# Output-gate projection of an mLSTM/S5 layer: plain float32 products replaced by three products of high and low parts

## The reference, cut to what matters

```python
xn = rmsnorm(h, norm1_g[l])
z = xn @ w_in[l]                       # 2048 x (4*1024 + 8 + 1024)
q, k, v, o, gates, u = jnp.split(z, [W, 2 * W, 3 * W, 4 * W, 4 * W + 2 * H], axis=-1)
qk = jax.nn.silu(causal_dwconv(jnp.concatenate([q, k], axis=-1), conv_qk_w[l]))
...
hm = mlstm_chunkwise(to_heads(q), to_heads(k), to_heads(v), li, lf)
hm = hm * lax.rsqrt(jnp.mean(hm * hm, axis=-1, keepdims=True) + RMS_EPS)
hm = hm.reshape(B, S, W) * mlstm_norm_g[l] * jax.nn.sigmoid(o)
ys = s5_groups(u, ...)
mix = jnp.concatenate([hm, ys], axis=-1) @ w_out[l]
```

## Time and profile before

| | us |
|---|---|
| median of 3 runs (lowest, highest) | 3444.53 (3444.41, 3446.69) |
| profiled execution, its own time | 3445.2 |
| its span | 3443.5 |
| busy: PE, DVE, ACT, POOL | 2603.8, 2528.7, 828.4, 1117.8 |

### The profile page before, as it was taken

How to read it: one execution, slowest core, us unless ns; L and a number is a source line. 1 busy time by engine, 2 the same in 40 slices (tenths; PEclk the granted TensorE clock), 3 DMA queues, 4 the chain that set the end, 5 groups by cost and what they waited for, 6 DMA issues and landing times. The chain is left out here.

```text
span 3443.5 us, 26884 instructions
## 1 busy us (share of the span) xinstructions
PE 2603.8 (76%) x10227; PEld 1778.2 (52%) x10227; DVE 2528.7 (73%) x2565; ACT 828.4 (24%) x794; POOL 1117.8 (32%) x654
## 2 busy tenths in 40 slices
PE   9999999625060600025558999999999999999999
PEld 4444674202020200012226888788788788888887
DVE  5997548889999999986676787679666544444565
ACT  2002231100000100000003333455433433333333
POOL 6550008786867687876660000000000000000000
PEclk9999999857575755557778999999999999999999
DMA  8885459999999999999997997454657555555775
GB/s 288 312 326 182 171 189 407 412 422 421 421 415 421 401 422 422 421 422 422 422 421 268 325 319 272 147 159 158 214 195 256 170 185 193 185 192 185 266 268 186
DMA packets 326003, 1023.36 MB, mean 297 GB/s; under 512 B 33784, under 2 KB 34312, under 8 KB 259212
## 3 DMA queue, kind: packets, MB, share of 16 engines
q1 hardware_dynamic: 251996, 484.97, 41.3%
q0 software_dynamic: 73904, 537.04, 37.6%
HBM read 1015.08 MB, written 6.86 MB: 297 GB/s over the span
## 5 line engine op out<-in xcount | busy, mean ns | idle before, releaser
L403 DVE TENSOR_TENSOR slab_low<-ring,slab_high 128x2048 fp32r<-128x2048 f32 x220 | 504.3, 2292 | 489.1 <-ACT slab_high L396 489.0
L396 ACT CAST slab_high<-ring 128x2048 fp32r<-128x2048 f32 x284 | 542.3, 1910 | 893.1 <-PE bank L382 722.8
L1996 POOL DMA_INDIRECT pool<-in_peer_u,pool x239 | 494.0, 2067 | 301.3 <-DVE pool L1722 202.0
L1772 DVE CUSTOM_DVE_ANT_0 pool<-pool,nat 128x2048 f32<-128x2048 f32 x235 | 535.0, 2291 | 42.9 <-DMA pool<-in_peer_u,pool 41.5
L380 PE MATMUL bank<-slab_high,left_high 128*128 128x512 f32 x1408 | 551.8, 392 | 11.7 <-DVE res L1810 6.3
L382 PE MATMUL bank<-slab_high,left_low 128*128 128x512 f32 x1408 | 549.6, 390 | 0.0
L381 PE MATMUL bank<-slab_low,left_high 128*128 128x512 f32 x1408 | 549.3, 390 | 0.0
L2507 PE MATMUL bank<-pool,causal 128*128 128x512 f32 x288 | 189.1, 818 | 424.3 <-ACT causal L2187 328.3
L1783 DVE SCALAR_TENSOR_TENSOR res<-pool,res 128x2048 f32<-128x2048 f32 x169 | 397.4, 2351 | 106.2 <-DMA pool<-in_peer_v,pool 92.7
L1996 POOL DMA_INDIRECT pool<-in_peer_v,pool x241 | 400.1, 1660 | 209.5 <-PE bank L2507 108.5
L2507 PEld LDWEIGHTS bank<-pool,causal 128*128 128x128 f32 x288 | 73.6, 266 | 538.2 <-issue 367.8
(11 more groups left out here) (628 smaller groups left out, 3341.0 us busy)
## 6 DMA issues: line engine op xcount, KB each, us to landing
ring<-in_w_in SPq DMA_DIRECT2D x141, 1024.0 KB, 5.2
ring<-in_w_ffn_in SPq DMA_DIRECT2D x88, 1024.0 KB, 5.0
ring<-in_w_ffn_out SPq DMA_DIRECT2D x44, 1024.0 KB, 5.1
nat<-in_w_ada SPq DMA_DIRECT2D x68, 512.0 KB, 5.6
ring<-in_w_out SPq DMA_DIRECT2D x32, 1024.0 KB, 5.1
left_scratch<-in_w_ada SPq DMA_DIRECT2D x60, 512.0 KB, 5.6
ring<-in_w_ada SPq DMA_DIRECT2D x23, 1024.0 KB, 5.5
ring<-in_peer_wq SPq DMA_DIRECT2D x10, 1024.0 KB, 5.1
```

Of the source, the lines that this page charges most:

```text
L396: nc.scalar.copy(high[:, n % PARTS], ring[:, g % SLOTS]).then_inc(high_done, 1)
L403: eng.tensor_tensor(dst, ring[:, g % SLOTS], high[:, n % PARTS].bitcast(F32), ALU.subtract)\
L1772: v.tensor_tensor_reduce(out=row, in0=row, in1=nat[:, t, :], scale=1.0, scalar=0.0, op0=ALU.mult, op1=ALU.add, accum_out=actv[:, t, m:m + ...
L1996: g.indirect_dma_start(dst, None, a[table][0], bass.IndirectOffsetOnAxis(idx[:, t, n:n + 1], 0))\
```

## The change

The eight slabs of the output gate are multiplied as three float32r products instead of plain float32.

- At the end of the first block ACT copies `raw_left` into a float32r array laid over `res` (two copies of 128 x 2048), and DVE subtracts it from `raw_left` in place (128 x 2048, 128 x 1024, 128 x 1024), each part once the last projection has read it. `left_high` so holds the low part of the left side.
- Each slab's high part is made in `slab_low` by a copy: slab 0 by ACT in the first block, slab 1 by POOL, slabs 2 to 7 by ACT, set between the other steps of its order.
- Each slab's low part is a subtraction on POOL, in place in the ring: slab 0 in the first block, the rest in the second.
- `res` is loaded again only when all eight slabs are used.

```diff
+        def o_high_part(eng, x):
+            g = O0 + x
+            eng.wait_ge(landed[slot_of(g)], reach[g])
+            if x >= PARTS:
+                eng.wait_ge(slabs_used, g - PARTS + 1)
+            if x == PARTS:
+                eng.wait_ge(low_done, x)
+            copy = nc.scalar.copy if eng is nc.scalar else nc.gpsimd.tensor_copy
+            copy(low[:, x % PARTS], slot(g)).then_inc(high_done, 1)
+
+        def o_low_part(x):
+            g = O0 + x
+            nc.gpsimd.wait_ge(high_done, x + 1)
+            nc.gpsimd.tensor_tensor(ring_low[:, slot_of(g)], slot(g), low[:, x % PARTS].bitcast(F32), ALU.subtract)\
+              .then_inc(low_done, 1)
...
 # first block, GpSimd, at its end
+                o_low_part(0)
 # first block, ScalarE, in front of taking the last projected block
+                            act.wait_ge(s_yp, SC)
+                            for ks in (slice(0, KD // 2), slice(KD // 2, KD)):
+                                nc.scalar.copy(o_left_high[:, ks, :], raw_left[:, ks, :]).then_inc(s_olh, 1)
+                            act.wait_ge(s_tab, SC)
+                            o_high_part(act, 0)
 # first block, VectorE, behind the scan
+                    for lo, hi in ((0, KD // 2), (KD // 2, KD - KS), (KD - KS, KD)):
+                        dve.wait_ge(s_olh, 1 if lo == 0 else 2)
+                        dve.wait_ge(slabs_used, place_of["in", (IN_BLOCKS - 3) * NB, hi // KS - 1] + 1)
+                        v.tensor_tensor(aTh[:, lo:hi, :], raw_left[:, lo:hi, :], o_left_high[:, lo:hi, :].bitcast(F32),
+                                        ALU.subtract)
 # second block, SyncE
-                stream_on(sp, O0, O0 + 4)
+                stream_on(sp, O0, len(front))
+                sp.wait_ge(slabs_used, len(front))
                 sp.dma_start(res, a["x"][0].rearrange("(t p) d -> p t d", p=P)).then_inc(s_x, 16)
-                stream_on(sp, O0 + 4, len(front))
                 sp.wait_ge(s_x, 16)
 # second block, GpSimd
+                o_high_part(g, 1)
+                o_low_part(1)
                 g.wait_ge(s_glub, 1)
                 g.wait_ge(s_cs, 1)
                 g.tensor_copy(condition, spread[:, :, 31]).then_inc(s_io, 1)
+                for x in range(PARTS, 8):
+                    o_low_part(x)
 # second block, ScalarE
                 for n in range(4, 8):
                     raw_copy(n)
-                for c in range(4):
+                o_high_part(act, 2)
+                for c in range(2):
+                    s5_sigmoid(c)
+                o_high_part(act, 3)
+                for c in range(2, 4):
                     s5_sigmoid(c)
...
+                o_high_part(act, 4)
                 for c in range(4, 6):
                     s5_sigmoid(c)
                 o_sigmoid(0)
+                o_high_part(act, 5)
                 for c in range(6, 8):
                     s5_sigmoid(c)
...
+                for x in range(6, 8):
+                    o_high_part(act, x)
                 act.wait_ge(s_m, mk["sq"])
 # second block, TensorE, o_slab(x)
-                    whole_slab(pe, O0 + x, [(ps[6 + t][:, :], t) for t in range(TT)], 4 * j, j == 0, j == 3)
+                    pe.wait_ge(low_done, x + 1)
+                    for k in range(KS):
+                        for t in range(TT):
+                            lh, ll = o_left(4 * j + k, t)
+                            hs, ls, into = low[:, x % PARTS, k, :], ring_low[:, slot_of(g), k, :], ps[6 + t][:, :]
+                            nc.tensor.matmul(into, lh, hs, start=j + k == 0, stop=False)
+                            nc.tensor.matmul(into, lh, ls, start=False, stop=False)
+                            last = nc.tensor.matmul(into, ll, hs, start=False, stop=(j, k) == (3, KS - 1))
+                    last.then_inc(slabs_used, 1)
```

More of the change, by code:

```diff
@@ L109, in build @@
         spare, _ = place_at("slab_low_scratch", PARTS * SLAB, F32, low_at)
-        res_, _ = place_at("res", TT * D)
+        res_, res_at = place_at("res", TT * D)
         aTh_, aT_at = place_at("left_high", KD * T, F32R)
@@ L216, in build @@
         place_of = {what: g for g, what in enumerate(front)}
+        O0 = place_of["in", (IN_BLOCKS - 2) * NB, 0]
         def front_slab(g, s):
@@ L278, in is_whole @@
             sec = max(i for i in range(len(SECTIONS)) if first_slab[i] <= g)
-            return sec in (FRONT, PEER_Q) or any(first_slab[i] <= g < first_slab[i] + WHOLE for i in (W_OUT, FFN_IN))
+            return g < O0 or sec == PEER_Q or any(first_slab[i] <= g < first_slab[i] + WHOLE for i in (W_OUT, FFN_IN))
         WHOLE = 2
@@ L288, in is_in_place @@
         def is_in_place(g):
-            return first_slab[GATES] <= g < first_slab[W_OUT2]
+            return first_slab[GATES] <= g < first_slab[W_OUT2] or O0 <= g < len(front)
         def split_index(g):
@@ L386, in left, with o_left @@
             return aTh[:, k, t * P:(t + 1) * P], aTl[:, k, t * P:(t + 1) * P]
+        o_left_high = view(place_at("o_left_high", KD * T, F32R, res_at)[0][:, :], [KD, T])
+        def o_left(k, t):
+            return o_left_high[:, k, t * P:(t + 1) * P], aTh[:, k, t * P:(t + 1) * P]
+        def o_high_part(eng, x):
[12 more added lines that the diff above has]
+              .then_inc(low_done, 1)
         def high_part(act, g, i=None):
@@ L597, in build @@
         U0 = place_of["in", C_U, 0]
+        s_olh = sem("o_left_high_copied")
         s_xp, s_rot, s_st, s_yp, s_yd = (sem("s5_inputs"), sem("s5_inputs_taken"), sem("s5_states"), sem("s5_outputs"),
@@ L600, in build @@
         s_proj, s_v5 = sem("qkv_taken"), sem("s5_vector_step")
-        O0 = place_of["in", (IN_BLOCKS - 2) * NB, 0]
         per_chunk = (O0 - S0) // SC
@@ L931, in s5 @@
                     for b in range(IN_BLOCKS - 2):
+                        if b == IN_BLOCKS - 3:
+                            act.wait_ge(s_yp, SC)
[3 more added lines that the diff above has]
+                            o_high_part(act, 0)
                         act.wait_ge(slabs_used, place_of["in", b * NB, 3] + 1)
```

## The result

The changed kernel takes 3457.99 us (median of 7 executions, 3456.17 to 3462.58) against 3444.41 of the kernel before on the same chip (7 executions, 3441.68 to 3446.69): a ratio of 1.0042, 95% interval 1.0033 to 1.0052. It is 13.6 us slower; 3457.4 was forecast. The profiled execution took 3457.99 with a span of 3456.3.

What follows compares the result with a forecast made beforehand. PE sets the pace, DVE close behind. Query-key products 15.1 us late less 4.3 returned (+10.8), restarts +1.5, first block +0.6: +12.9 on 3445.2 gives 3458.1, median 0.7 lower, 3457.4 us; 8-in-10 range 3442 to 3465.

Steps and rivals of the forecast that it cites:

- Rivals 1 and 2: 1: POOL doesn't hold DVE, 3436.2 us, chance 0.13; 2: two convolution low parts fall into DVE's waits or bank reads, 3448.2, 0.15.
- rival 3: Heavier: both restarts at the low clock, POOL's copy at 4.6 us, low parts at 5.5; about +20, 3465 us, chance 0.12.
- two restarts: PE resumes at the lower clock after waiting at `s5_glu(1)` and `s5_glu(6)`; +1.5 us together, range 0 to 3.7.
- Rival 4: PE waits for POOL's low parts themselves; no time beyond that of rival 3, chance 0.03.
- PE's saving: Output gate's slabs: 5.45 us as three products instead of 6.87, 1.42 saved each, 11.4 for eight if nothing else were late.
- ceiling of 8.9: Most PE could keep, even with free splitting: 4.6 us up to the query-key products plus 4.3 from slabs 5 to 7.
- POOL's durations: Second-block POOL work: each 128x2048 low-part subtraction 4.6 us (3.8 to 5.5), the one copy 3.0 (1.8 to 4.6).
- What DVE loses: DVE stopped in `glu_blk` and convolution for whole POOL instructions: copy 3.0 plus four low parts at 4.6, 21.4 us.
- DVE's waits: DVE's own waits before the last convolution instruction shrink by 3.2 us, leaving that instruction 18.2 late.
- The Silus: ACT after the convolution: three of four Silus done early, one of 1.1 us follows instead of a 3.1 us batch; -2.0.
- The first block's end: Slab 0's split on ACT and POOL delays DVE's last subtraction, so the copy at L1132 starts late; +0.6 us.
- At nothing: Zero cost expected from ACT's six high parts, input `x` issued last, slab transfers and the final DVE steps.

Runs made afterwards that it cites:

- one-column kernel: The changed kernel with POOL's eight low-part subtractions cut to the first column of each 512, high part multiplied instead; 3434.78 us against 3444.17 before the change.
- kernel with the memsets: The changed kernel with POOL's low parts of slabs 1 to 7 replaced by three memsets each, high part multiplied instead; 3444.57 us, ratio 0.9998 to the kernel before.

## Why the prediction was right

The forecast of 3457.4 stands 0.6 us from the measured median; its case, DVE held for the whole length of POOL's subtractions, is shown by three runs: cut their length and 23 us go, add them alone and 16 come, take their reads away and the convolution's two-operand steps are at 5.09 again. Rivals 1 and 2 fall with that. Of rival 3 the two restarts at the lower clock came true, the higher prices of POOL's work did not. Rival 4 falls by PE's waits, which name no low part. Step by step:

- **PE's saving.** Right: eight records of `s5_glu` and the slab behind them took 336.48 - 327.88 = 8.60 us before and 345.33 - 338.12 = 7.21 after, 1.39 less for the 1.42 of the sum, and slabs 5 to 7 gave back 17.8 - 13.6 = 4.2 for 4.3. The busy time is no witness: it fell by 4.3 us in the stage, since records at the lower clock took about 7.3 more (transposes 1.6, `s5_glu` 1.0 and 1.9, slab 1 1.8, slab 4 1.0). The one-column kernel reached 8.4 of the ceiling of 8.9.
- **POOL's durations.** The subtraction 4.5 to 4.6 uncontended, as taken from half of it in the earlier trace rows. The copy 1.89 for 3.0: at the bottom of its range. In the one-column kernel, where a DVE step stood in front of it, it is 2.74.
- **What DVE loses.** Forecast 21.4, measured 5.83 in `glu_blk` + 4.25 + 8.55 = 18.6. The two instructions of `glu_blk` take 2.62 and 5.63 us (1.2 each when alone). The first is held by the copy for 1.4 us, the second by low part 1 for 4.4. So of the missing 2.8, 1.6 is the copy, taken at 3.0, and 1.2 the four low parts, which cost 4.25 to 4.4 each, not 4.6. The places were right: low parts 1, 2, 4 and 5 hit, 3, 6 and 7 do not (low part 1 fell into `glu_blk`, not behind it).
- **DVE's waits.** They were to shrink by 3.2. The last convolution instruction ends at 368.25, 18.8 late; less the 18.6 and the block's start (1.6 late) the waits shrank by 1.4. The rest is the clock: slab 1 took 7.2 us instead of 5.45 behind PE's first long wait, and DVE waits 2.82 us at 339.60 for a sigmoid whose product PE does behind that slab. The two restarts were put down at +1.5; this one comes to 1.8, and the other, at slab 4, ends as the last Silu does and adds 0.2.
- **The Silus.** Wrong: -2.0 was taken for three of the four being done early. They ran as one batch again:

```profile
365.61 0.38 ACT L2078 ACTIVATE parts_scratch<-bank 128x256 f32<-128x256 f32 x1 [1.32 <-PE bank L2312]
367.31 3.91 ACT L2117 ACTIVATE pool<-pool 128x1024 f32<-128x1024 f32 x4
```

  ACT does its steps in order, and the last sigmoid in front of the Silus waits for `s5_glu(7)`, which PE finishes only at 365.6, behind its 9.1 us wait and at half clock. A wait of PE on DVE passed through PE to ACT: the walk had looked at DVE and ACT, and not at what ACT's queue holds in front of the Silus. In the sum these 2 us stand against the 2.8 by which the blocking was overcounted. But PE shows no wait in front of the query-key products: the last Silu ends at 371.22, and slab 4, begun at the lower clock, ends at 371.4. Two paths tie there, and three Silus done early would not have let PE start sooner. The prediction had the one path through the last Silu only.
- **The first block's end.** Forecast +0.6, measured +1.6. ACT's high part 0 waited 0.97 us for its slab to land and ended at 300.73, not at 299.5; so POOL's subtraction ended at 305.41, not 304.1, and DVE's copy started at 306.41, 1.63 late. (In the kernel before, PE's slab at 293.81 took 8.19 us, in the changed one 7.13; without that the lag would be up to 1 us larger, an estimate from these two.) Missed as well is the barrier behind it: PE idles 4.3 us there, and its transposes run at the lower clock, 3.52 us for the 1.96 of before. The kernel with slab 0's low part on DVE keeps both away; 1.6 us of it reach the stage's end.
- **At nothing.** ACT's high parts, input `x` (SP issues it at 406.91 and nothing waits for it) and the last DVE steps: no wait shows any of them.

From the block's start to the last transposes the sum had +12.3 (10.8 and 1.5), and 12.0 is measured; with the start, 13.6 for 12.9, and 12.8 at the end of the profile. Up to the query-key products the terms missed by -2.8 (blocking), +1.8 (DVE's waits, which hold the first restart), -1.5 (the restarts, booked apart), +1.9 (Silus) and +0.2 (slack): 16.6 became 16.2. The agreement to 0.6 us is better than the terms deserve; that much of it is luck.

## What to carry to other kernels

Before elementwise work goes to an idle GpSimd, look at what VectorE does in the same microseconds. Beside VectorE steps with two SBUF operands a GpSimd subtraction cost VectorE 91% to 94% of its own length, 4.25 us, while the same subtraction on VectorE took 2.28; beside copies from PSUM banks it cost nothing, and a placement that is free in one schedule need not be in the next. And a product made cheaper on an engine that leads by one microsecond is worth only what the next engine leaves: here the three slabs behind the last wait on VectorE gave 4 us, and splitting all eight on VectorE gave none that the times show.

## What the runs showed of the hardware

- GpSimd's memsets, which read nothing, stop VectorE's one-operand TENSOR_SCALAR (128 x 256 x 4: 1.14 us alone, 5.21 beside them) and leave its SCALAR_TENSOR_TENSOR with two operands at 5.09. The Trainium skill, SBUF — State Buffer, section "Who interferes with whom", says that a VectorE instruction with two SBUF inputs contends with a GpSimd one that reads SBUF and not with one that only writes, and that `tensor_scalar` can run in a mode that contends with GpSimd. The runs agree with both; in which mode the TENSOR_SCALAR ran they don't show.
- GpSimd's copy, which reads one operand, holds VectorE's two-operand TENSOR_TENSOR too: 4.05 us for 2.35 in the one-column kernel, beside the copy.
- GpSimd's copy of 128 x 2048 to float32r took 1.89 us, its subtraction 4.5, and a subtraction with the same array as both operands 3.6.
- Behind some waits TensorE's granted clock was at the lower of its two levels: 0.50 of full speed from 361.8 to 365.0, behind 9.1 us, where eight records of `s5_glu` took 3.78 us instead of 1.89 and slab 4 then 6.4 instead of 5.45; 0.50 from 327.6 to 332.0, behind 7.2 us, where slab 1 took 7.2; 0.56 from 308.2 to 311.5, behind 4.3 us at the barrier, where sixteen transposes took 3.52 us instead of 1.96.
- The length of the wait alone does not tell which level follows: behind 2.2 us the transposes took 1.97 us in the kernel with slab 0's low part on VectorE, while behind 2.0 us eight records of `s5_glu` took 3.65, at a granted clock of 0.50, in the kernel with the memsets.
